# Mixer B of a hybrid decoder step: bias loads moved ahead of each stage's last loop turn, one group merge moved into the next round's first GEMM, small cache copies spread over the FFN stages

## The chip, the cores and the metric

The kernel runs on one core of one Trainium2 chip. The metric is the device time of one execution in microseconds (us); lower is better. Engine names are those of the profile: PE is TensorE (PEld its weight loads), DVE is VectorE, ACT is ScalarE, POOL is GpSimd, SP is SyncE, which here only issues DMAs.

## The reference

One inference step of a two-layer decoder over 512 prompt tokens and 8 x 4 sampled tokens, all in float32. Each layer is a half-step SwiGLU FFN, a token mixer and a second half-step FFN, each followed by a LayerNorm. Layer 0 has mixer A (sliding-window attention with sinks), layer 1 has mixer B: three groups of heads with window and dilation (128, 1), (512, 4) and (2048, 16), whose outputs are combined by their softmax denominators.

```python
for i in range(DEPTH):                      # DEPTH = 2
    xp, xs = half_ffn(xp, i, 0, 0), half_ffn(xs, i, 0, 0)
    ...                                     # mixer A (i = 0) or mixer B (i = 1)
    xp, xs = post_norm(xp, yp, i, 1), post_norm(xs, ys, i, 1)
    xp, xs = half_ffn(xp, i, 1, 2), half_ffn(xs, i, 1, 2)

def mixer_b_prompt(x, w_qkv, w_o, table):
    qkv = (x @ w_qkv).reshape(b, s, N_GROUPS_B, 3, N_HEADS, HEAD_DIM)
    for gi, (w, d) in enumerate(DILATED_GROUPS):
        ...                                 # banded attention with stride d: o and log-sum-exp
    y = combine_groups(outs, lses).reshape(b, s, -1) @ w_o

def combine_groups(outs, lses):
    w = jax.nn.softmax(jnp.stack(lses, 0), axis=0)
    return jnp.einsum('gnth,gnthd->nthd', w, jnp.stack(outs, 0))
```

For the sampled tokens, the caches of past keys and values (the oldest four rows dropped, four new ones appended) are outputs too. So nearly all cache bytes are copied from input to output in HBM: the long ones (groups 2 and 3 of mixer B) and the small ones, 128 rows per sequence (group 1 of mixer B, 8 KB a row, and mixer A, 2 KB a row).

## The kernel before

All work is laid out by hand, engine by engine, with semaphores between the engines. The work is a list of phases: for each layer `up`, `down`, `qkv`, `wo`, `up`, `down`. A phase is a row of units. One unit is one weight tile of 128 output columns: SP loads it into one of four buffers `raw` (`load_unit`, DMA lines L555, L559, L564), ACT casts it into `wh` (L1215), DVE takes the rest into `wl` (L1476), and PE multiplies with both (L777, L779, L781), 48 matmuls of 272 columns in two PSUM banks. A buffer `raw[j]` is free again when the unit's `wl` is made; SP waits for that (`wl_rdy`) before each load. SP's queue is in program order, so whatever stands ahead of a load holds it up.

Mixer B has two rounds (8 heads each). A round has two stages. The first is a GEMM of 12 units for group 1 and its attention, the second a GEMM of 24 units for groups 2 and 3 and their attention. Round 0 is `qkv[1, 0, 0]` and `qkv[1, 0, 1]`, round 1 is `qkv[1, 1, 0]` and `qkv[1, 1, 1]`. Below they are stage 1, 2, 3 and 4. In a GEMM of a stage, PE transposes each finished tile (L920, and L921 for the sampled tokens' 32 columns, once a tile), DVE and ACT in turn stage the tile and keep the transposed part (`stage_tile`, `keep_tokens`). Each attention (`attention(ps, rn)`) needs a bias of 1 MB in `RB["bias"]`; the buffer is single, so `load_bias` waits until the attention before it has added its last bias.

After a round's second attention the two slots `RB["o"][0]` and `RB["o"][1]` are merged: POOL sends each slot's maxima and denominators through HBM to swap their token order (`exchange`, `fetch`), DVE and ACT make the weights (`weights(k)`, L1634 to L1647), and `outputs_b(r)` puts features on partitions. PE transposes four pairs (L1018, 8 transposes each, into banks 6 and 7), ACT copies bank 6 (L1366), DVE adds bank 7 (L1667), and PE waits for that before it starts the next pair.

For each of the four mixer B stages SP does this before:

```python
load_bias(pass_b[2 * ph.run.rnd + (ph.run.items[0][1] > 0)])
n0 = 4 * ph.run.rnd + 2 * (ph.run.items[0][1] > 0)
keep_small(1, n0, n0 + 2)
keep_small(0, n0, n0 + 2)
load_units(ph, 1)
```

Units 0 to 3 are loaded before that (`load_first`). `keep_small` copies the small caches of two sequences, from HBM to HBM. The long caches are copied in the FFN phases, one DMA behind each weight load (`keep`, `keep_rows`, L539). The four `up` phases have 44 units each, eleven loop turns of four.

Of the kernel before, what the change touches and what calls it, by code (L numbers as in the profile page):

```python
# [20 lines left out]
P = 128  # L21
D_MODEL = 1024
KC = D_MODEL // P
SEQ = 512
NS = 8
DEC = 4
# [6 lines left out]
DEPTH = 2  # L33
# [74 lines left out]
def build(nc, t, o):  # L108
# [4 lines left out]
    with ExitStack() as ctx:  # L113
# [412 lines left out]
        def _(sp):  # L526
# [13 lines left out]

            def keep_small(layer, n0, n1):

                src = caches[layer, 0][0, n0:n1].rearrange("n r w h d -> n (r w h d)")
                dst = states_s[layer, 0][0, n0:n1].rearrange("n r w h d -> n (r w h d)")
                row = 2 * LAYER[layer]["kv"] * HD
                total = src.shape[1]
                sp.dma_start(dst[:, 0:total - DEC * row], src[:, DEC * row:total]).then_inc(copy_done[2 * DEPTH], 16)

# [35 lines left out]

            def load_units(ph, first):
                with sp.Fori(first, ph.units // RAW) as it:
                    for j in range(RAW):
                        load_unit(ph, it, j)
                        keep(ph, it, j)
                    if ph is up[0, 0]:  # L590
                        sp.wait_ge(line_o, 32)
                        repeat_lines(it * LINE_ROWS, LINE_ROWS)
# [126 lines left out]
            for ph in phases:  # L719
                if ph is qkv[0]:  # L720
                    load_qkv_a(ph, range(RAW))
                    load_bias(pass_a)
                    load_qkv_a(ph, range(RAW, ph.units))
                elif ph.kind == "qkv":
                    if not peeled:
                        load_first(ph)
                    load_bias(pass_b[2 * ph.run.rnd + (ph.run.items[0][1] > 0)])
                    n0 = 4 * ph.run.rnd + 2 * (ph.run.items[0][1] > 0)
                    keep_small(1, n0, n0 + 2)
                    keep_small(0, n0, n0 + 2)  # L730
                    load_units(ph, 1)
                else:
                    if ph.kind == "down" and ph.l == 0:
                        load_first(ph)
                        if ph.f == 0:
                            load_norms()
                            repeat_lines(LINE_ITS * LINE_ROWS, P - LINE_ITS * LINE_ROWS)
                        load_decode_constants(ph.f)
                        for j in range(RAW):
                            keep(ph, 0, j)  # L740
                        load_units(ph, 1)
                    else:
                        load_units(ph, peeled)
# [15 lines left out]
            for f in range(2 * DEPTH):  # L759
                sp.wait_ge(copy_done[f], 16 * RAW * (UP_ITS + DOWN_ITS))  # L760
            sp.wait_ge(copy_done[2 * DEPTH], 16 * 2 * 4)
            sp.wait_ge(new_done, 16 * 4)
# [8 lines left out]
        def _(pe):  # L771
# [338 lines left out]
            for ph in phases:  # L1110
# [10 lines left out]
                elif ph.kind == "qkv":  # L1121
                    qkv_run(ph, n_norm)
                    if ph is qkv[0]:
                        attention(pass_a, ph.run)
                        outputs_a()
                        decode(0)
                    else:
                        r, y = ph.run.rnd, int(ph.run.items[0][1] > 0)
                        attention(pass_b[2 * r + y], ph.run)
                        if y:  # L1130
                            outputs_b(r)
                            if r:
                                pe.wait_ge(sp_l, 2)
                                decode(1)
                            else:
                                pe.wait_ge(ot_v, PAIRS + 4)
                else:
# [72 lines left out]
        def _(act):  # L1210
# [94 lines left out]
            def run(ph):  # L1305
                r = ph.run
                for i in range(r.n):
# [50 lines left out]
            def outputs_b(r):  # L1358
# [3 lines left out]
                for p_ in range(4):  # L1362
                    act.wait_ge(ot_done, PAIRS + 4 * r + p_ + 1)
                    if p_ >= 2:
                        act.wait_ge(ot_v, PAIRS + 4 * r + p_ - 1)
                    act.copy(RB["st"][p_ % 2][:, 0:SEQ], bank[6][:]).then_inc(ot_a, 1)  # L1366
                if r:
# [72 lines left out]
            for ph in phases:  # L1440
                if ph.kind == "qkv":
# [6 lines left out]
                    else:  # L1448
                        r, y = ph.run.rnd, int(ph.run.items[0][1] > 0)
                        attention(pass_b[2 * r + y], ph.run)  # L1450
                        if y:
                            weights(1 + 2 * r)
                            weights(2 + 2 * r)
                            outputs_b(r)
                            if r:
                                decode(1)
                elif ph.kind == "up":
# [11 lines left out]
        def _(dve):  # L1469
# [110 lines left out]
            def run(ph):  # L1580
                r = ph.run
                for i in range(r.n):
# [45 lines left out]
            def weights(k):  # L1628
# [29 lines left out]
            def outputs_b(r):  # L1658
# [3 lines left out]
                for p_ in range(4):  # L1662
                    dve.wait_ge(ot_a, PAIRS + 4 * r + p_ + 1)
                    v = RB["at"][:, p_, :].rearrange("p (u c) -> p u c", c=4)
                    y = bank[7][:].rearrange("p (c u) -> p u c", c=4)
                    x = RB["st"][p_ % 2][:, 0:SEQ].rearrange("p (u c) -> p u c", c=4)
# [163 lines left out]
            for ph in phases:  # L1830
                if ph.kind == "qkv":
# [13 lines left out]
                    else:  # L1845
                        r, y = ph.run.rnd, int(ph.run.items[0][1] > 0)
                        attention(pass_b[2 * r + y], ph.run)
                        if y:
                            ps = pass_b[2 * r + 1]
                            dve.wait_ge(st_done, ps.u0 + ps.units)  # L1850
                            dve.wait_ge(oev_done, ps.u0 + ps.units + 2)
                            weights(1 + 2 * r)
                            weights(2 + 2 * r)
                            outputs_b(r)
                            if r:
                                decode(1)
                elif ph.kind == "up":
# [227 lines left out]
```

## Time and profile before

| | before |
|---|---|
| time, median of 3 runs | 3385.55 us (3382.94 to 3388.15) |
| the profiled execution | 3389.92 us, span 3388.1 us |
| PE busy | 2939.0 us, 87% of the span |
| PEld busy | 2669.2 us, 79% |
| DVE, ACT, POOL busy | 1286.1, 895.1 and 820.6 us (38%, 26%, 24%) |
| mean granted PE clock | 0.918 |
| DMA | 482.09 MB; SP's queue takes 42.0% of 16 engines' span |
| time on this kernel's four mixer B stages (from 1696 to 2538 us) | about 842 us |

PE is busy for most of the span, so the time hangs on its pauses. The four FFN stretches show hardly any. The page's slices of granted clock dip in the mixer stages and in the two decodes. How each pause came about is read from the waits, the timeline of an engine, and the DMAs.

### The profile page before, as it was taken

The numbers are of one execution on the slowest core, as the hardware profiler recorded it, in microseconds if no ns is written. First come the engines' busy times: TensorE is split into PE (matmuls) and PEld (weight loads), VectorE is DVE, ScalarE is ACT, GpSimd is POOL, SyncE is SP. The second block draws the span as 40 slices with busy tenths as digits, with TensorE's granted clock in tenths as the row PEclk, the third lists the DMA queues.
The fourth block names the chain that finished last, engine by engine and source line by source line (L and its number), as shares of the span: only waits on it lengthen the run. The fifth ranks groups of instructions, "written<-read, shape, count | busy, mean of one in ns | idle before, by whom it ended". The sixth has DMA issues, their size and how long they took to land. (4 is left out here: it accounts for less than half of the span.)

```text
span 3388.1 us, 53741 instructions
## 1 busy us (share of the span) xinstructions
PE 2939.0 (87%) x20802; PEld 2669.2 (79%) x20802; DVE 1286.1 (38%) x1934; ACT 895.1 (26%) x1725; POOL 820.6 (24%) x834
## 2 busy tenths in 40 slices
PE   8999998548999999999968696786964787899998
PEld 7999987417899999999967696776952222899998
DVE  2222244673422224222234123341258665422223
ACT  2222123432222222222124123131233341322212
POOL 2222012251222202222012123111226552122210
PEclk9999999758999999999979898898975888999999
DMA  7666431003566535665221231213305676366651
GB/s 244 228 236 180 154 82 30 17 15 93 187 206 200 186 124 180 208 207 186 90 94 52 95 108 54 76 54 100 107 8 174 245 278 250 101 206 206 211 170 49
DMA packets 466743, 482.09 MB, mean 142 GB/s; under 512 B 60878, under 2 KB 439871, under 8 KB 462448
## 3 DMA queue, kind: packets, MB, share of 16 engines
q1 hardware_dynamic: 456584, 467.46, 42.0%
q0 software_dynamic: 6416, 12.20, 1.3%
q8 instruction: 85, 1.39, 0.2%
q10 hardware_dynamic: 3616, 0.69, 0.1%
q14 instruction: 42, 0.34, 0.0%
HBM read 466.46 MB, written 199.42 MB: 197 GB/s over the span
## 5 line engine op out<-in xcount | busy, mean ns | idle before, releaser
L777 PE MATMUL bank<-sb_xh,sb_wl 128*128 128x272 f32 x4416 | 962.6, 295 | 124.8 <-DVE sb_wl L1476 102.5
L781 PE MATMUL bank<-sb_xh,sb_wh 128*128 128x272 f32 x4416 | 949.4, 292 | 0.0
L779 PE MATMUL bank<-sb_xl,sb_wh 128*128 128x272 f32 x4416 | 946.2, 291 | 0.0
L1476 DVE TENSOR_TENSOR sb_wl<-sb_raw,sb_wh 128x1024 fp32r<-128x1024 f32 (+1 forms) x340 | 453.4, 1334 | 1109.5 <-ACT sb_wh L1215 1100.9
L777 PEld LDWEIGHTS bank<-sb_xh,sb_wl 128*128 128x128 f32 x4416 | 717.4, 192 | 133.3 <-issue 76.1
L779 PEld LDWEIGHTS bank<-sb_xl,sb_wh 128*128 128x128 f32 x4416 | 717.8, 192 | 0.7
L781 PEld LDWEIGHTS bank<-sb_xh,sb_wh 128*128 128x128 f32 x4416 | 712.3, 192 | 0.0
L1215 ACT CAST sb_wh<-sb_raw 128x1024 fp32r<-128x1024 f32 (+1 forms) x340 | 376.5, 1110 | 1048.5 <-PE bank L781 939.3
L1898 POOL CAST sb_hh<-sb_h 128x544 f32 x88 | 130.2, 1480 | 758.2 <-DVE sb_h L1485 758.2
L777 PE MATMUL bank<-sb_hh,sb_wl 128*128 128x272 f32 x1408 | 311.4, 292 | 0.0
L781 PE MATMUL bank<-sb_hh,sb_wh 128*128 128x272 f32 x1408 | 304.2, 288 | 0.0
L779 PE MATMUL bank<-sb_hl,sb_wh 128*128 128x272 f32 x1408 | 303.7, 287 | 0.0
L777 PEld LDWEIGHTS bank<-sb_hh,sb_wl 128*128 128x128 f32 x1408 | 226.4, 188 | 2.0
L779 PEld LDWEIGHTS bank<-sb_hl,sb_wh 128*128 128x128 f32 x1408 | 225.8, 188 | 0.5
L781 PEld LDWEIGHTS bank<-sb_hh,sb_wh 128*128 128x128 f32 x1408 | 225.1, 188 | 0.0
L2005 POOL TENSOR_TENSOR sb_dprb<-sb_dkvb,sb_dqbb 128x1024 f32<-128x1024 f32 x64 | 168.1, 2639 | 108.1 <-ACT sb_dqbb L1386 71.1
L1485 DVE TENSOR_TENSOR sb_h<-sb_sil,bank 128x272 f32<-128x272 f32 x176 | 69.0, 433 | 267.8 <-PE bank L781 267.8
L1039 PE MATMUL bank<-sb_dq2b,sb_pick 128*128 128x512 f32 x192 | 93.5, 563 | 73.5 <-ACT sb_dqbb L1386 54.9
L1039 PEld LDWEIGHTS bank<-sb_dq2b,sb_pick 128*128 128x128 f32 x192 | 39.2, 225 | 148.3 <-ACT sb_dqbb L1386 113.1
L1222 ACT ACTIVATE sb_sil<-bank 128x272 f32<-128x272 f32 x88 | 35.0, 398 | 441.6 <-PE bank L781 441.6
L1069 PE MATMUL bank<-sb_dkvb,sb_dpb 128*16 128x512 f32 x384 | 139.0, 680 | 12.7 <-DMA sb_dkvb<-in_cache_b_kv 12.0
L1781 DVE TENSOR_REDUCE sb_dsb<-sb_dprb 128x16 f32<-128x1024 f32 x96 | 114.8, 1217 | 58.1 <-POOL sb_dprb L2005 56.9
(244 smaller groups left out, 2774.1 us busy)
## 6 DMA issues: line engine op xcount, KB each, us to landing
out_state_b_s<-in_cache_b_kv SPq DMA_DIRECT2D x176, 704.0 KB, 6.2
sb_dkvb<-in_cache_b_kv SPq DMA_DIRECT2D x144, 512.0 KB, 5.7
sb_raw<-in_ffn_w_gate SPq DMA_DIRECT2D x88, 512.0 KB, 3.8
sb_raw<-in_ffn_w_up SPq DMA_DIRECT2D x88, 512.0 KB, 4.2
sb_raw<-in_ffn_w_down SPq DMA_DIRECT2D x64, 704.0 KB, 4.6
sb_raw<-in_attn_b_w_qkv SPq DMA_DIRECT2D x72, 512.0 KB, 3.9
out_state_b_s<-in_cache_b_kv SPq DMA_DIRECT2D x32, 1016.0 KB, 7.6
out_state_b_s<-in_cache_b_kv SPq DMA_DIRECT2D x4, 1984.0 KB
```

Source lines behind the costliest of these rows:

```text
L777: pe.matmul(acc(s, h), wl[slot][:, k, :], hi(k)[:, halves[h]], start=start and k == 0, stop=False)
L779: pe.matmul(acc(s, h), wh[slot][:, k, :], lo(k)[:, halves[h]], start=False, stop=False)
L781: last = pe.matmul(acc(s, h), wh[slot][:, k, :], hi(k)[:, halves[h]], start=False, stop=end)
L1039: pe.matmul(bank[c][:], pick[:, tok:tok + 1].to_broadcast([P, P]), D["q2"][:, y.g, c * 512:(c + 1) * 512], start=True, stop=True).then_inc ...
L1069: mm = pe.matmul(bank[2 + 4 * (n % 2) + c][32 * tau:32 * tau + HEADS, 0:w], D["p"][:, g, n * DEC + tau, :], D["kv"][x.slot][:, c * w:(c + ...
L1215: act.copy(wh[j % 2][:, 0:ph.chunks, :], raw[j][:, 0:ph.chunks, :]).then_inc(wh_rdy, 1)
L1222: act.activation(sil[b][:, halves[0]], acc(0, 0), ACT.Silu)
L1476: dve.tensor_tensor(wl[j % 2][:, 0:ph.chunks, :], raw[j][:, 0:ph.chunks, :], v.bitcast(F32), ALU.subtract).then_inc(wl_rdy, 1)
L1485: last = dve.tensor_tensor(h32[b][:, halves[h]], sil[b][:, halves[h]], acc(1, h), ALU.mult)
L1781: dve.tensor_reduce(D["s"][:, y.g, tok * HEADS:(tok + 1) * HEADS], D["pr"][y.slot][:].rearrange("p (h d) -> p h d", d=HD), AX_X, ALU.add). ...
L1898: pool.tensor_copy(hi, h32[b][:]).then_inc(hh_rdy, 1)
L2005: pool.tensor_tensor(D["pr"][y.slot][:].rearrange("p (k r d) -> p k r d", r=rep, d=HD), kk, D["qb"][y.slot][:].rearrange("p (k r d) -> p k ...
```

## The change

Three things are changed.

1. In the mixer stages the bias is loaded before the last loop turn's four weight units, and no longer behind the first four units. In mixer A (a stage of 12 single units) it moves from behind unit 3 to behind unit 7.
2. `keep_small` is gone. `keep_window` copies the same rows in pieces: eleven rows of two sequences of both small caches at the end of each turn of an `up` phase, and the last three rows in the `down` phase. All `down` phases now load their first four units ahead of their copies.
3. Round 0's merge is taken out of the end of stage 2. Its weights are made by DVE and ACT in stage 3's GEMM, behind tiles 3 and 6, and `outputs_b(0)` runs behind that GEMM, ahead of stage 3's attention. In both rounds `outputs_b` now uses banks 6 and 7 for even pairs and banks 4 and 5 for odd ones, and PE waits only for the pair before the last.

```diff
-            def keep_small(layer, n0, n1):
-
-                src = caches[layer, 0][0, n0:n1].rearrange("n r w h d -> n (r w h d)")
-                dst = states_s[layer, 0][0, n0:n1].rearrange("n r w h d -> n (r w h d)")
-                row = 2 * LAYER[layer]["kv"] * HD
-                total = src.shape[1]
-                sp.dma_start(dst[:, 0:total - DEC * row], src[:, DEC * row:total]).then_inc(copy_done[2 * DEPTH], 16)
+            def keep_window(ffn, r0, rows):
+
+                n = slice(2 * ffn, 2 * ffn + 2)
+                for layer in range(2):
+                    src = caches[layer, 0][0, n].rearrange("n r w h d -> n r (w h d)")[:, bass.ds(r0 + DEC, rows), :]
+                    dst = states_s[layer, 0][0, n].rearrange("n r w h d -> n r (w h d)")[:, bass.ds(r0, rows), :]
+                    sp.dma_start(dst, src).then_inc(copy_done[2 * DEPTH], 16)
...
+            def load_units(ph, first, end=None):
+                with sp.Fori(first, end or ph.units // RAW) as it:
                     for j in range(RAW):
                         load_unit(ph, it, j)
                         keep(ph, it, j)
+                    if ph.kind == "up":
+                        keep_window(ph.ffn, it * LINE_ROWS, LINE_ROWS)
...
                 elif ph.kind == "qkv":
                     if not peeled:
                         load_first(ph)
+                    last = ph.units // RAW - 1
+                    load_units(ph, 1, last)
                     load_bias(pass_b[2 * ph.run.rnd + (ph.run.items[0][1] > 0)])
-                    n0 = 4 * ph.run.rnd + 2 * (ph.run.items[0][1] > 0)
-                    keep_small(1, n0, n0 + 2)
-                    keep_small(0, n0, n0 + 2)
+                    load_units(ph, last, last + 1)
...
             def outputs_b(r):
                 pe.wait_ge(ow_rdy, NBLK + 8 * (r + 1))
                 for p_ in range(4):
-                    if p_:
-                        pe.wait_ge(ot_v, PAIRS + 4 * r + p_)
+                    if p_ >= 2:
+                        pe.wait_ge(ot_v, PAIRS + 4 * r + p_ - 1)
...
-                            mm = pe.transpose(bank[6 + y][:, b * P:(b + 1) * P], RB["o"][y][:, b, p_ * P:(p_ + 1) * P], ident[:])
+                            mm = pe.transpose(bank[6 - 2 * (p_ % 2) + y][:, b * P:(b + 1) * P], RB["o"][y][:, b, p_ * P:(p_ + 1) * P], ident[:])
...
+                        if r and not y:
+                            for b in range(2):
+                                pe.wait_ge(tr_free[b], (ph.run.tr0 + ph.run.n) // 2 + 2)
+                            outputs_b(0)
+                            pe.wait_ge(ot_v, PAIRS + 4)
                         attention(pass_b[2 * r + y], ph.run)
-                        if y:
-                            outputs_b(r)
-                            if r:
-                                pe.wait_ge(sp_l, 2)
-                                decode(1)
-                            else:
-                                pe.wait_ge(ot_v, PAIRS + 4)
+                        if r and y:
+                            outputs_b(1)
+                            pe.wait_ge(sp_l, 2)
+                            decode(1)
...
+                    if ph is qkv[1, 1, 0] and i in (3, 6):
+                        weights(i // 3)
...
+                    if ph is qkv[1, 1, 0] and i in (3, 6):
+                        group_weights(0, i // 3 - 1)
...
+            def group_weights(r, y):
+
+                ps = pass_b[2 * r + 1]
+                dve.wait_ge(st_done, ps.u0 + ps.units)
+                dve.wait_ge(oev_done, ps.u0 + ps.units + 2)
+                weights(1 + 2 * r + y)
```

The first addition with `i in (3, 6)` is ACT's, the second DVE's. The order of the instructions on three engines follows. Line numbers are those of each kernel's own file, so a line that did not change has another number in the change.

**SP, stage 1 of mixer B, before.** The four loads of the first row are units 0 to 3, `sb_biasb` is the bias, L547 are the two small copies (the shape is that of the whole transfer, in float32 elements), and the last rows begin the loop over the other units.

```order
L564 DMA sb_raw<-in_attn_b_w_qkv 128x8x128 x4
L636 DMA sb_biasb<-scr_lines_x 128x8x256
L547 DMA out_state_b_s<-in_cache_b_kv 2x16x15872
L547 DMA out_state_a_s<-in_cache_a_kv 2x4x15872
L586 UNCONDITIONAL_BRANCH
L586 ISA
L564 ISA
L564 DMA sb_raw<-in_attn_b_w_qkv 128x8x128
```

**SP, the same place in the change.** Each row of four loads is one turn.

```order
L564 DMA sb_raw<-in_attn_b_w_qkv 128x8x128 x4
L586 UNCONDITIONAL_BRANCH
L564 DMA sb_raw<-in_attn_b_w_qkv 128x8x128 x4
L586 REGISTER_ALU
L586 COMPARE_AND_BRANCH
L638 DMA sb_biasb<-scr_lines_x 128x8x256
L586 UNCONDITIONAL_BRANCH
L564 DMA sb_raw<-in_attn_b_w_qkv 128x8x128 x4
```

The two copies have left the stage, and units 4 to 7 stand ahead of the bias.

**SP, the end of a turn of an `up` phase, in the change.** Before, the turn ends with the copy of L539 behind the fourth load.

```order
L555 DMA sb_raw<-in_ffn_w_up 128x8x128
L539 ISA
L539 DMA out_state_b_s<-in_cache_b_kv 16x11264
L547 ISA x2
L547 DMA out_state_a_s<-in_cache_a_kv 2x5632
L547 ISA
L547 DMA out_state_b_s<-in_cache_b_kv 2x2x11264
L586 REGISTER_ALU
```

The long copy is laid out as 16 pieces, the two new ones have the two sequences as their outermost dimension.

**DVE, from stage 2's last attention rows on, before.** L1612 is the attention's output, L1634 to L1647 are one slot's weights, L1667 the sums of `outputs_b`, L1476 makes `wl` of the next GEMM (stage 3). The second slot's weights, the same nine rows, are left out.

```order
L1612 COPY sb_ob<-bank 128x128 x3
L1634 TENSOR_TENSOR sb_tb<-sb_mdb,sb_mob 128x32
...
L1647 TENSOR_TENSOR sb_ob<-sb_ob,sb_tb 128x512 x4
...
L1667 TENSOR_TENSOR sb_at<-bank,sb_stb 128x512 x4
L1476 TENSOR_TENSOR sb_wl<-sb_raw,sb_wh 128x1024 x2
L1181 COPY sb_stb<-bank 128x272
```

**DVE, stage 3's GEMM in the change.** L1483 makes `wl`, L1185 to L1208 are `stage_tile` and `keep_tokens`, L1643 to L1656 a slot's weights.

```order
L1483 TENSOR_TENSOR sb_wl<-sb_raw,sb_wh 128x1024 x2
L1185 COPY sb_stb<-bank 128x272
L1186 COPY sb_stb<-bank 128x272
L1208 COPY sb_ssb<-bank 32x128
L1643 TENSOR_TENSOR sb_tb<-sb_mdb,sb_mob 128x32
...
L1656 TENSOR_TENSOR sb_ob<-sb_ob,sb_tb 128x512 x4
L1483 TENSOR_TENSOR sb_wl<-sb_raw,sb_wh 128x1024 x2
```

One slot's weights now stand between tile 3's copies and the `wl` of units 5 and 6; the other slot's stand between the `wl` of unit 7 and that of unit 8.

**PE, from stage 2's attention (L992) into stage 3's GEMM, before.**

```order
L976 MATMUL bank<-sb_ident,sb_stb 128x128 x4
L992 MATMUL bank<-sb_vb,sb_ktb 128x128 x8
L1018 MATMUL bank<-sb_ident,sb_ob 128x128 x32
L777 MATMUL bank<-sb_xh,sb_wl 128x272 x2
L779 MATMUL bank<-sb_xl,sb_wh 128x272 x2
```

**PE, from stage 3's last transposes of tiles (L922, L923) into its attention (L968), in the change.**

```order
L922 MATMUL bank<-sb_ident,sb_stb 128x128 x4
L923 MATMUL bank<-sb_ident,sb_stb 32x128
L1020 MATMUL bank<-sb_ident,sb_ob 128x128 x32
L968 MATMUL bank<-sb_kb,sb_qsb 128x128 x2
L968 MATMUL bank<-sb_kb,sb_qsb 128x256 x2
```

The 32 transposes of round 0's merge have moved from the head of stage 3's GEMM to its end.

## Rows read from the trace of the kernel before

**Rows 1.** Waits from 1696 to 2876 us: total us, times, longest us.

```profile
ACT sb_wh L1215 <- DMA sb_raw<-in_attn_b_w_qkv: 87.2, 6, 30.2
PE bank L777 <- DVE sb_wl L1476: 77.6, 5, 26.5
PE bank L1018 <- DVE sb_ob L1647: 42.6, 2, 29.8
```

**Rows 2.** PE's timeline around unit 4 of stages 1, 2 and 4.

```profile
1735.16 0.27 PE L921 MATMUL bank<-sb_ident,sb_stb 128*32 128x128 f32 x1
...
1765.84 0.27 PE L921 MATMUL bank<-sb_ident,sb_stb 128*32 128x128 f32 x1
...
1772.40 0.27 PE L921 MATMUL bank<-sb_ident,sb_stb 128*32 128x128 f32 x1
...
1886.74 0.27 PE L921 MATMUL bank<-sb_ident,sb_stb 128*32 128x128 f32 x1
...
1922.60 0.27 PE L921 MATMUL bank<-sb_ident,sb_stb 128*32 128x128 f32 x1
...
2298.64 0.27 PE L921 MATMUL bank<-sb_ident,sb_stb 128*32 128x128 f32 x1
...
2333.14 0.27 PE L921 MATMUL bank<-sb_ident,sb_stb 128*32 128x128 f32 x1
```

**Rows 3.** DMAs issued 1702.5 to 1703.5 us: KB each, median us to landing.

```profile
sb_raw<-in_attn_b_w_qkv SPq DMA_DIRECT2D x1, 512.0 KB, 51.5
```

**Rows 4.** DMA queue, 1709 to 1748 us: packets, MB, share of 16 engines.

```profile
q1 hardware_dynamic: 36, 2.16, 12.8%
```

**Rows 5.** Windows 902 to 926 and 2101 to 2131 us: busy times, PEclk, DMA share, GB/s.

```profile
902.00:926.00 24.00, 24.00 (x194) 24.00 (x193) 6.42 (x9) 5.34 (x8) 6.04 (x4) 1.00 0.62 208
2101.00:2131.00 30.00, 0.26 (x2) 0.28 (x3) 8.59 (x25) 0.70 (x4) 1.30 (x2) 0.54 0.21 76
```

**Rows 6.** PE's timeline, into stage 2 and into stage 3.

```profile
1861.07 0.49 PE L777 MATMUL bank<-sb_xh,sb_wl 128*128 128x272 f32 x2 [0.54 <-issue]
...
1873.62 0.27 PE L921 MATMUL bank<-sb_ident,sb_stb 128*32 128x128 f32 x1
...
2098.97 2.03 PE L992 MATMUL bank<-sb_vb,sb_ktb 128*128 128x128 f32 x16
...
2134.08 1.97 PE L1018 MATMUL bank<-sb_ident,sb_ob 128*128 128x128 f32 x8 [1.40 <-DVE sb_at L1667]
...
2158.43 0.27 PE L921 MATMUL bank<-sb_ident,sb_stb 128*32 128x128 f32 x1
```

**Rows 7.** DVE's timeline, weights of round 0 and stage 3's tile 3.

```profile
2120.86 0.19 DVE L1634 TENSOR_TENSOR sb_tb<-sb_mdb,sb_mob 128x32 f32<-128x32 f32 x1 [19.54 <-DMA sb_mob<-scr_md]
...
2125.69 0.18 DVE L1634 TENSOR_TENSOR sb_tb<-sb_mdb,sb_mob 128x32 f32<-128x32 f32 x1
...
2171.33 0.44 DVE L1181 COPY sb_stb<-bank 128x272 f32<-128x272 f32 x1 [3.56 <-PE bank L781]
...
2172.47 1.40 DVE L1476 TENSOR_TENSOR sb_wl<-sb_raw,sb_wh 128x1024 fp32r<-128x1024 f32 x1 [0.16 <-ACT sb_wh L1215]
```

**Rows 8.** PE's timeline, the start of stage 3's attention.

```profile
2228.68 1.89 PE L966 MATMUL bank<-sb_kb,sb_qsb 128*128 128x128 f32 x8 [3.26 <-POOL sb_qsb L1963]
```

**Rows 9.** ACT's and DVE's timelines, a pair of `outputs_b(1)`.

```profile
2532.85 0.59 ACT L1366 COPY sb_stb<-bank 128x512 f32<-128x512 f32 x1 [2.79 <-PE bank L1018]
...
2533.47 0.69 DVE L1667 TENSOR_TENSOR sb_at<-bank,sb_stb 128x512 f32<-128x512 f32 x1 [2.68 <-ACT sb_stb L1366]
```

**Rows 10.** DMAs issued 858 to 1120 us, an `up` phase: KB each, us to landing.

```profile
out_state_b_s<-in_cache_b_kv SPq DMA_DIRECT2D x38, 704.0 KB, 6.2
sb_raw<-in_ffn_w_gate SPq DMA_DIRECT2D x19, 512.0 KB, 3.8
```

**Rows 11.** SP's issue and ACT's cast of the same buffer in an `up` turn.

```profile
902.39 0.38 SPq L555 DMA_DIRECT2D sb_raw<-in_ffn_w_gate  x1
...
923.93 1.05 ACT L1215 CAST sb_wh<-sb_raw 128x1024 fp32r<-128x1024 f32 x1
```

More of the change, by code:

```diff
@@ L583, in keep @@
                     keep_rows(2, 2 * ph.ffn + j % 2, it * DOWN_ROWS + UP_ITS * 2 * UP_ROWS, DOWN_ROWS, ph.ffn)
-            def load_units(ph, first):
-                with sp.Fori(first, ph.units // RAW) as it:
+            def load_units(ph, first, end=None):
+                with sp.Fori(first, end or ph.units // RAW) as it:
                     for j in range(RAW):
@@ L720, in _ @@
                 if ph is qkv[0]:
-                    load_qkv_a(ph, range(RAW))
+                    load_qkv_a(ph, range(2 * RAW))
                     load_bias(pass_a)
-                    load_qkv_a(ph, range(RAW, ph.units))
+                    load_qkv_a(ph, range(2 * RAW, ph.units))
                 elif ph.kind == "qkv":
@@ L726, in _ @@
                         load_first(ph)
+                    last = ph.units // RAW - 1
+                    load_units(ph, 1, last)
                     load_bias(pass_b[2 * ph.run.rnd + (ph.run.items[0][1] > 0)])
-                    n0 = 4 * ph.run.rnd + 2 * (ph.run.items[0][1] > 0)
-                    keep_small(1, n0, n0 + 2)
-                    keep_small(0, n0, n0 + 2)
+                    load_units(ph, last, last + 1)
+                elif ph.kind == "down":
+                    load_first(ph)
+                    if ph.l == 0 and ph.f == 0:
+                        load_norms()
+                        repeat_lines(LINE_ITS * LINE_ROWS, P - LINE_ITS * LINE_ROWS)
+                    if ph.l == 0:
+                        load_decode_constants(ph.f)
+                    keep_window(ph.ffn, UP_ITS * LINE_ROWS, BLK - DEC - UP_ITS * LINE_ROWS)
+                    for j in range(RAW):
+                        keep(ph, 0, j)
                     load_units(ph, 1)
                 else:
[L733 to L741, printed above, removed]
-                    else:
-                        load_units(ph, peeled)
+                    load_units(ph, peeled)
                 peeled = int(ph.kind == "qkv")
@@ L760, in _ @@
                 sp.wait_ge(copy_done[f], 16 * RAW * (UP_ITS + DOWN_ITS))
-            sp.wait_ge(copy_done[2 * DEPTH], 16 * 2 * 4)
+            sp.wait_ge(copy_done[2 * DEPTH], 16 * 2 * 2 * DEPTH * (UP_ITS + 1))
             sp.wait_ge(new_done, 16 * 4)
@@ L1365, in outputs_b @@
                         act.wait_ge(ot_v, PAIRS + 4 * r + p_ - 1)
-                    act.copy(RB["st"][p_ % 2][:, 0:SEQ], bank[6][:]).then_inc(ot_a, 1)
+                    act.copy(RB["st"][p_ % 2][:, 0:SEQ], bank[6 - 2 * (p_ % 2)][:]).then_inc(ot_a, 1)
                 if r:
@@ L1449, in _ @@
                         r, y = ph.run.rnd, int(ph.run.items[0][1] > 0)
+                        if r and not y:
+                            outputs_b(0)
                         attention(pass_b[2 * r + y], ph.run)
[L1451 to L1456, printed above, removed]
+                        if r and y:
+                            weights(3)
+                            weights(4)
+                            outputs_b(1)
+                            decode(1)
                 elif ph.kind == "up":
@@ L1664, in outputs_b @@
                     v = RB["at"][:, p_, :].rearrange("p (u c) -> p u c", c=4)
-                    y = bank[7][:].rearrange("p (c u) -> p u c", c=4)
+                    y = bank[7 - 2 * (p_ % 2)][:].rearrange("p (c u) -> p u c", c=4)
                     x = RB["st"][p_ % 2][:, 0:SEQ].rearrange("p (u c) -> p u c", c=4)
@@ L1846, in _ @@
                         r, y = ph.run.rnd, int(ph.run.items[0][1] > 0)
+                        if r and not y:
+                            outputs_b(0)
                         attention(pass_b[2 * r + y], ph.run)
[L1848 to L1856, printed above, removed]
+                        if r and y:
+                            group_weights(1, 0)
+                            group_weights(1, 1)
+                            outputs_b(1)
+                            decode(1)
                 elif ph.kind == "up":
```

1 line of the change is left out of this document (removed).

## The prediction

> **What bounds the kernel now.** I began with the waits of PE, since PE is busy 87% of the span and everything else has room. In the stretch of mixer B three waits stand out [rows 1]. PE waits 77.6 us for `wl` of a GEMM, five times, the longest 26.5. It waits 42.6 us for the merged slots, twice, the longest 29.8. And ACT, which makes `wh` ahead of `wl`, waits 87.2 us for weights to land. So the first wait is not DVE's or ACT's work: it is a late DMA. PE's timeline gives the place. One L921 ends each tile, and in a steady GEMM they are 6.56 us apart (1765.84 to 1772.40). Around unit 4 of stages 1, 2 and 4 the distance is 30.68, 35.86 and 34.50 us [rows 2]. Stage 3 has no such gap, as it begins with the merge.
>
> Then the DMAs. The load of unit 4 stands behind the bias and the two small copies, and landed 51.5 us after its issue [rows 3], where the weight loads of an `up` phase take 3.8 [rows 10]. Between 1709 and 1748 us SP's queue moved 36 packets, 2.16 MB, at 12.8% of 16 engines [rows 4]. That is two engines of 16, about 60 KB a packet, 55.4 GB/s together or 27.7 GB/s each. The two copies hold 1984 + 496 = 2480 KB, 1240 KB for each of two engines, which at 27.7 GB/s is 45.8 us. The weight tile is spread over all 16, so it is whole only when the two slow engines come to it. This explains all three gaps, and in stage 3 the copies lie under the merge wait.
>
> **The change part by part.**
>
> *Copies out of the mixer stages, loads ahead of the bias.* Unit 4's load needs only unit 0's buffer, which is free before PE starts the stage's GEMM, and nothing is left in front of it. I take the three gaps down to the steady distance: 30.68 - 6.56 = 24.1, 35.86 - 6.56 = 29.3, 34.50 - 6.56 = 27.9 [rows 2]. These differences also hold what the first GEMM after a pause loses on a lower clock. Sum 81.3 us. The bias now comes with the last turn, four units (26 us) ahead of its attention. It is 1 MB, twice a weight tile, so two to three times 3.8 us: its cover is at least twice that. If it were late the DVE, and with it PE, would wait for the difference. The bounds are 0 (something else holds unit 4) and 81.3.
>
> *Round 0's merge.* Stage 2's attention ends at 2098.97 + 2.03 = 2101.00 and the first L921 of stage 3 is at 2158.43, 57.43 us later. At the border of stages 1 and 2, where nothing is merged, it is from 1861.07 - 0.54 = 1860.53 to 1873.62, 13.09 us [rows 6]. So 57.43 - 13.09 = 44.3 us leave this place. Some of it comes back:
>
> (a) `outputs_b(0)` behind stage 3's GEMM. PE idles 3.26 us there anyway, while POOL stages the queries [rows 8]. A pair is 8 transposes, 1.97 us [rows 6] at a granted clock near half (0.54 in the idle stretch before, [rows 5]), so about 1.1 at full clock, then ACT's copy 0.59 and DVE's sum 0.69 [rows 9], with some 0.1 us per handover. With the last tile's copy ahead (0.8 us), pairs 0 and 1 go at once, pair 2 starts when pair 0 is summed (3.4 us), pair 3 at 4.5 and ends 2.6 later: 7.1 us, less the 3.26 that were idle, +3.9. Bounds: 0, and 11.0 if nothing overlaps (0.8 + 4 x 3.37 - 3.26, with 1.97 + 1.40 of [rows 6]).
>
> (b) The weights in the GEMM. One slot takes DVE 2125.69 - 2120.86 = 4.83 us. Tile 3's GEMM ends at 2171.3, its copies take to 2172.4, and then `wl` of unit 5 took 1.2 to 1.4 us [rows 7]. With a slot between, `wl` is there 1.1 + 4.8 + 1.25 = 7.15 us after the tile's end, and PE wants it after 6.56 + 0.3: late by 0.3. What is queued behind it on DVE (tile 5's copies) has a unit's time. The second slot begins earlier, behind unit 7's `wl`, but needs ACT's exponentials, and ACT stands at tile 6's staging until that GEMM ends. By the same count `wl` of unit 8 comes 6.9 us after tile 6, late by 0.1. Sum +0.5, bounds 0 and 2 x 4.83 = 9.7.
>
> So 44.3 - 3.9 - 0.5 = 39.9.
>
> *`outputs_b(1)` with four banks.* Before, four pairs of 1.97 + 1.40 = 3.37 us, 13.5 [rows 6]. Here PE is slow after its wait, so the transposes come one behind the other, 4 x 1.97 = 7.9, plus the last pair's 0.59 + 0.69 and handovers: 9.3. Decode waits for the end of it: 4.2 us gained; bounds 0 and 5. The wait ahead (the second of [rows 1], 12.8 of the 42.6) stays.
>
> *Copies in the `up` phases.* Per turn two more DMAs, from 22 rows of 8 KB and 22 rows of 2 KB. They are issued with the two sequences outermost, as the old ones were, so I charge them to two engines: 110 KB each, 112.6 KB at 27.7 GB/s = 4.1 us per turn. A turn lasts 24 us with a DMA share of 0.62 [rows 5], or 14.9 us of each engine; with 4.1 it is 19.0, so no backlog is carried over. A load issued at 902.39 lands 3.8 later, and its buffer's next cast is at 923.93 [rows 10, 11]: 17.7 us of cover against 4.1. I take 0. If that cover were gone it would cost up to 44 turns x 4.1 = 179 us. Two more issues on SP, about 0.7 us each, fit into its waits. The long copies, spread over 16 engines, land in 6.2 us [rows 10] and nobody waits for them.
>
> The Trainium skill, *DMA: Bandwidth & Descriptors*, section "Why a DMA increments its semaphore by 16 and not by 1", says that the number of engines follows from the slowest dimension other than 1 of both access patterns, the largest divisor up to 16. By that rule a leading 2 means two engines, and the trace agrees for the old copies (12.8% of 16). It speaks against the change, since the new ones have it too, always on the same two engines. The sum would be the same by it, unless the cover in the `up` phases fails.
>
> *Mixer A's bias behind unit 7* is covered, as PE has no gap there now: 0. *Down phases*: four loads ahead of their copies, 0.
>
> **Sum.** 81.3 + 39.9 + 4.2 = 125.4 us. The profiled execution took 3389.9 us (span 3388.1 and 1.8 around it): 3264.5. It lies 4.4 us above the median of the runs, 3385.55, so I forecast **3260 us**.
>
> **Rivals.**
>
> *The merge is not hidden* (bounds of (a) and (b)): DVE's two slots stand fully in PE's way and the pairs run one by one: +7.1 and +9.2 us, 3276. For it: DVE has hardly 4 us of slack per unit. Against: the count above leaves PE only 0.4 late. Chance 7%.
>
> *Something else holds unit 4.* The change takes the copies away and the loads stay late, say because SP stands at another semaphore. Then only the merge and the banks count: 3385.6 - 44.1 = 3341. Against: the 51.5 us are from issue to landing, not before the issue. Chance 3%.
>
> *Slower: the small copies hold the weights of the `up` phases.* Two engines get 4.1 us more per turn on top of 14.9. Should each turn stand by more than 125.4 / 44 = 2.85 us, the change loses; with the whole 4.1 on the path the time is 3260 + 179 = 3439. That needs loads to land more than 20 us after issue, and the rows give 3.8. Chance 2%.
>
> *Forecast case*: 87%, own range 3250 to 3270. The rest, 1%, is no change.
>
> **The range.** From 3250 (nothing comes back from (a) and (b), and 5 us of run-to-run and size) to 3280, which takes in the first rival. Faster by over 0.2% (7 us, about what a measurement of this kernel can tell from none) 0.97, same 0.01, slower 0.02.
>
> **What would show it.** Right: L921 every 6.56 us through units 3 to 5 of all four stages; unit 4's load landing in about 4 us; no wait of PE for ACT's or DVE's data of 20 us; stage 3's first L921 13 us after stage 2's attention; between stage 3's last tile and its scores some 7 us with 32 transposes; `up` turns still 24 us. Wrong: a gap of PE at units 5 or 8 of stage 3 over 1 us, gate or up loads that land later than 15 us, or a wait of DVE for the bias ahead of an attention.

## The result, and the profile after

The changed kernel takes **3258.09 us** (median of 4 runs, 3254.3 to 3262.15); the kernel before, run beside it on the same chip, 3385.12 us (3382.94 to 3388.15). The ratio is 0.9622, its 95% interval 0.961 to 0.9634: 127 us less. The profiled execution took 3262.15 us with a span of 3260.3 us, where before had 3389.92 and 3388.1; its mean granted clock is 0.939 (0.918).

The waits of PE in mixer B, 1696 to 2746 us (columns as in [rows 1]):

```profile
PE bank L978 <- ACT sb_stb L1336: 20.1, 29, 1.7
PE bank L1041 <- DVE sb_dq2b L1694: 17.0, 1, 17.0
PE bank L1020 <- DVE sb_ob L1656: 12.9, 1, 12.9
...
PE bank L963 <- POOL sb_qsb L1977: 8.7, 2, 4.4
...
PE bank L779 <- DVE sb_wl L1483: 3.9, 3, 2.0
```

Against [rows 1]: the wait for `wl` has gone from 77.6 to 3.9 us, that for the merged slots from 42.6 in two pieces to 12.9 in one. ACT's 87.2 us for weights to land has no row left in this stretch. L923 is the L921 of [rows 2]; PE's timeline of stage 1:

```profile
1728.78 0.27 PE L923 MATMUL bank<-sb_ident,sb_stb 128*32 128x128 f32 x1
1735.34 0.27 PE L923 MATMUL bank<-sb_ident,sb_stb 128*32 128x128 f32 x1
1741.90 0.27 PE L923 MATMUL bank<-sb_ident,sb_stb 128*32 128x128 f32 x1
```

Every 6.56 us, where [rows 2] has 30.68 at this place. The DMAs issued from 1698 to 1740 us show why, 3.7 us instead of the 51.5 of [rows 3], and the bias beside them:

```profile
sb_raw<-in_attn_b_w_qkv SPq DMA_DIRECT2D x5, 512.0 KB, 3.7
sb_biasb<-scr_lines_x SPq DMA_DIRECT2D x1, 1024.0 KB, 6.9
```

PE's timeline from the last product of stage 2 into stage 3, the only pause in that GEMM (unit 5), and from its last transposes into the attention:

```profile
2045.30 2.03 PE L994 MATMUL bank<-sb_vb,sb_ktb 128*128 128x128 f32 x16
2047.86 0.49 PE L779 MATMUL bank<-sb_xh,sb_wl 128*128 128x272 f32 x2 [0.54 <-issue]
...
2060.39 0.27 PE L923 MATMUL bank<-sb_ident,sb_stb 128*32 128x128 f32 x1
...
2080.70 0.52 PE L779 MATMUL bank<-sb_xh,sb_wl 128*128 128x272 f32 x2 [0.35 <-DVE sb_wl L1483]
...
2127.73 0.27 PE L923 MATMUL bank<-sb_ident,sb_stb 128*32 128x128 f32 x1
2128.87 1.94 PE L1020 MATMUL bank<-sb_ident,sb_ob 128*128 128x128 f32 x16 [0.87 <-DVE sb_ssb L1208]
2131.34 1.97 PE L1020 MATMUL bank<-sb_ident,sb_ob 128*128 128x128 f32 x16 [0.53 <-DVE sb_at L1683]
2134.71 1.58 PE L968 MATMUL bank<-sb_kb,sb_qsb 128*128 128x128 f32 x8 [1.40 <-DVE sb_at L1683]
```

From the end of the attention (2047.33) to the first L923 it is 13.06 us, where [rows 6] has 57.43. The merge's 32 transposes go in two groups of 16: two pairs at once, then each after the sum of the one before the last.

In an `up` phase the windows show the window copies as a somewhat larger DMA share, 0.64 at 882 to 906 us where [rows 5] has 0.62 for a like turn. The DMAs issued from 858 to 1120 us, with their queue's total (packets, MB, share of 16 engines):

```profile
q1 hardware_dynamic: 46935, 52.53, 59.9%
...
out_state_b_s<-in_cache_b_kv SPq DMA_DIRECT2D x38, 704.0 KB, 6.2
...
out_state_b_s<-in_cache_b_kv SPq DMA_DIRECT2D x10, 176.0 KB
out_state_a_s<-in_cache_a_kv SPq DMA_DIRECT2D x10, 44.0 KB
```

Against [rows 10], the long copies land as before, and the gate weights in 4.0 us instead of 3.8.

**The balance of the two spans**, from the first and the last matmul of each stage in both timelines: GEMMs of stages 1, 2 and 4: -24.1, -29.3 and -28.0; stage 3's border and GEMM -43.8; from there to its attention +3.4, and that attention -2.1; stage 4's attention -1.7; from its end to the decode -5.1; the decode, from its first to its last product of queries and cached keys, +2.9. Sum -127.8 = 3260.3 - 3388.1. The parts that are not listed moved as well, by up to 2 us each (the last `up` GEMM -1.9, mixer A's attention -1.4), and cancel.

### The profile page after: what moved, and what is told of

It reads as the page before. It is cut to its first block and busy times, and to the rows that moved or that the text cites. A ratio compares the mean times of both kernels' runs of the same rounds, so it can differ in the third digit from the quotient of the medians.

```text
span 3260.3 us, 54005 instructions
## 1 busy us (share of the span) xinstructions
PE 2920.5 (90%) x20802; PEld 2648.9 (81%) x20802; DVE 1284.9 (39%) x1934; ACT 894.0 (27%) x1725; POOL 817.0 (25%) x834
## 5 line engine op out<-in xcount | busy, mean ns | idle before, releaser
L1483 DVE TENSOR_TENSOR sb_wl<-sb_raw,sb_wh 128x1024 fp32r<-128x1024 f32 (+1 forms) x340 | 453.0, 1333 | 1001.7 <-ACT sb_wh L1219 992.8
```

The costliest lines, as they stand in the source:

```text
L1483: dve.tensor_tensor(wl[j % 2][:, 0:ph.chunks, :], raw[j][:, 0:ph.chunks, :], v.bitcast(F32), ALU.subtract).then_inc(wl_rdy, 1)
```

## The experiments

Times are medians; "before" beside each is its run on the same chip.

**The copies alone.** In the kernel before, `keep_small` gives way to `keep_window` in the FFN stages; bias, merge and banks stay.

```diff
+                    if ph.kind == "up":
+                        keep_window(ph.ffn, it * LINE_ROWS, LINE_ROWS)
...
                     load_bias(pass_b[2 * ph.run.rnd + (ph.run.items[0][1] > 0)])
...
-                    keep_small(1, n0, n0 + 2)
-                    keep_small(0, n0, n0 + 2)
                     load_units(ph, 1)
...
```

> The kernel before with only the small copies moved into the FFN phases; the bias is still ahead of unit 4, the merge and the banks are as before. Theory (the two-engine copies held unit 4's load): the gaps of stages 1, 2 and 4 go (-81.3 us), and round 0's merge wait falls from 29.8 us to the 12.9 of round 1, since its exchange through HBM is not held either (-16.9): about 3385 - 98 = 3287 us, 3280 to 3295. Rival (the bias, or SP's wait for it ahead of unit 4, holds the load): the gaps stay in full or in half, 3330 us or more.

Measured: 3286.56 us (before 3387.52), ratio 0.9713 (0.9697 to 0.973): 101 us less. All GEMM gaps are gone. Of the two merge waits round 0's is shorter, 16.2 us instead of 29.8 (I had expected 12.9); round 1's stays at 12.8:

```profile
PE bank L1020 <- DVE sb_ob L1649: 29.0, 2, 16.2
```

**The copies stay, but spread over 16 engines.** One DMA for each sequence; source and target are then one row of numbers each, without the dimension of two sequences.

```diff
-                src = caches[layer, 0][0, n0:n1].rearrange("n r w h d -> n (r w h d)")
+                for n in range(n0, n1):
+                    src = caches[layer, 0][0, n].rearrange("r w h d -> (r w h d)")
...
```

> The kernel before with each small copy issued per sequence, 16 pieces each (992 KB and 248 KB), in the same place ahead of unit 4. Theory (it is the two engines, not the bytes or the place): 2480 KB over 16 engines at 27.7 GB/s are 5.7 us, unit 4's load lands within about 15 us, well inside its 26 us: as the copies-only kernel, 3287 us, 3280 to 3300. Rival (2.4 MB of HBM traffic ahead of the load is the cause, wherever it runs): unit 4 late as before, 3370 us or more.

Measured: 3291.89 us (before 3387.52), ratio 0.9728 (0.971 to 0.9745): 96 us less without moving a DMA. The same bytes stand in front of unit 4's load, and it lands 11 us after its issue. The DMAs issued from 1700 to 1712 us:

```profile
sb_raw<-in_attn_b_w_qkv SPq DMA_DIRECT2D x2, 512.0 KB, 11.4
out_state_b_s<-in_cache_b_kv SPq DMA_DIRECT2D x1, 992.0 KB, 9.2
```

The packets of the large copy have the same size in both traces, 63,488 bytes. Before, they run two at a time, each 2.34 us long, from 1705 to 1752 us; here 16 start between 1701.9 and 1703.4 us. So it was the two engines that held the weights, not the bytes, the packets or the order as such. It stays 5 us above the copies-alone run; 4 of the 5 are in the merge waits, 33.1 us in sum instead of 29.0.

**The merge alone**, with its four banks; SP's part as before.

```diff
+                        if r and not y:
...
+                            outputs_b(0)
...
-                    if p_:
-                        pe.wait_ge(ot_v, PAIRS + 4 * r + p_)
+                    if p_ >= 2:
+                        pe.wait_ge(ot_v, PAIRS + 4 * r + p_ - 1)
```

> The change without its SP part: merge in stage 3's GEMM and four banks, copies and bias ahead of unit 4 as before. Theory (in stage 3 the copies' hold lay under the merge wait): a gap of 25 to 29 us appears at unit 4 of stage 3. The gain is 44.3 - 4.4 + 4.2 - 27.9 = 16 us: 3369 us, 3360 to 3376. Rival (the parts add up one by one): -44, 3341 us.

Measured: 3367.5 us, ratio 0.995 (0.9934 to 0.9967): 20 us less. The merge leaves the place where it hid stage 3's copies, and unit 4 of stage 3 now waits like that of the other stages:

```profile
2151.46 0.81 PE L777 MATMUL bank<-sb_xh,sb_wl 128*128 128x272 f32 x2 [25.57 <-DVE sb_wl L1481]
```

Its GEMM is 27 us longer than in the change (105.55 us, 78.49).

**The order alone.** Bias and both small copies, laid out as before, ahead of the last loop turn.

```diff
+                    last = ph.units // RAW - 1
+                    load_units(ph, 1, last)
                     load_bias(pass_b[2 * ph.run.rnd + (ph.run.items[0][1] > 0)])
                     keep_small(1, n0, n0 + 2)
                     keep_small(0, n0, n0 + 2)
-                    load_units(ph, 1)
+                    load_units(ph, last, last + 1)
```

> The kernel before with bias and whole small copies together moved ahead of the last loop turn; nothing else. Theory: the two slow engines now hold the first unit of the last turn (unit 8 or 20). It is issued some 4 us after the tile six units before it ended, lands 51 us later and is wanted 39.7 us after that tile's end: a gap of about 18 us in each of the four stages, 72 us in place of 81.3, and the merge wait falls by 16.9: 3359 us, 3345 to 3375. Rival (the place of the bias was what held the loads): gaps gone, 3287 us or less.

Measured: 3378.36 us (10 runs), ratio 0.9976 (0.9966 to 0.9985). The prediction took copies and order as one step; of the order alone only 9 us come. The gaps move to the first unit of the last turn, 19.4, 22.3, 20.5 and 22.8 us, and there are four of them, stage 3's too. With what PE loses behind them (last section) the four GEMMs are 93.5 us longer than steady ones, more than the 81.4 of before; what is gained is round 0's merge wait, 12.8 us instead of 29.8. My 3359 missed by 19: I had expected 72 us for the four gaps, they are 85.0, and 8.5 us come behind them. The load behind the copies still takes long:

```profile
sb_raw<-in_attn_b_w_qkv SPq DMA_DIRECT2D x1, 512.0 KB, 47.2
```

**SP's part whole**, the copies in the FFN stages and the bias ahead of the last turn, on the other engines of before. The edit is the SP part of the change's diff.

> The whole of the change's SP part (copies in the FFN stages, bias ahead of the last loop turn) on the kernel before's other engines: both merges stay as they were, with two banks. It differs from the run with the copies alone (3286.56 us) only in the place of the bias. Theory (the bias behind units 0 to 3 holds nobody once the copies behind it are gone, and ahead of the last turn it holds nobody either): within 3 us of that run, 3284 to 3290, ratio to before 0.970 to 0.972, no gap of PE in the GEMMs. Rival: 1 MB of bias in front of the last four weight tiles makes the first of them late: some 5 us in each stage, 3300 or more, with a PE gap at the first unit of the last turn.

Measured: 3286.81 us (before 3386.32), ratio 0.9709 (0.9696 to 0.9722), as the copies alone: the time shows nothing of the bias's place. The profile shows where the prediction's split was off. PE's wait for round 0's merge is no longer the 29.8 of [rows 1]; the first row is of PE, the second of DVE, from 2040 to 2075 and 2040 to 2080 us:

```profile
PE bank L1020 <- DVE sb_ob L1649: 12.7, 1, 12.7
```

```profile
DVE sb_tb L1636 <- DMA sb_mob<-scr_md: 2.5, 1, 2.5
```

In [rows 7] DVE waited 19.54 us for the same `sb_mob`, which comes over HBM behind stage 3's copies. That wait is 2.5 here: 17 us of the merge wait were not the merge's. Most of them go with the copies alone, where DVE waits 5.9 us and PE 16.2; the last 3.4 go with the bias and unit 4's load, which with the copies alone are issued beside this exchange (at 2038.5 and 2039.2 us) and with SP's part whole are not. Other parts of the two kernels differ by as much, so the time doesn't show them.

**Two banks.** The change, with `outputs_b` on banks 6 and 7 alone and a wait for each pair.

```diff
-                    if p_ >= 2:
-                        pe.wait_ge(ot_v, PAIRS + 4 * r + p_ - 1)
+                    if p_:
+                        pe.wait_ge(ot_v, PAIRS + 4 * r + p_)
...
```

> The change with the old outputs_b: two banks, each pair waits for the one before; the merge stays behind stage 3's GEMM. Theory: in stage 3 a pair takes about 1.1 + 1.4 = 2.5 us on the full clock, 10 us in place of 7.1, +3; in round 1 the 4.2 us come back. So 3258 + 7 to 8 = 3266 us, 3260 to 3271. Rival (PE's end of the pairs is hidden behind POOL's and ACT's work): 3258, no difference.

Measured: 3267.18 us (before 3387.55), ratio 0.965 (0.9634 to 0.9666), 9 us above the change. PE's timeline has the 3.37 us pitch of [rows 6] back:

```profile
2125.99 1.97 PE L1020 MATMUL bank<-sb_ident,sb_ob 128*128 128x128 f32 x8 [1.40 <-DVE sb_at L1683]
2129.36 1.97 PE L1020 MATMUL bank<-sb_ident,sb_ob 128*128 128x128 f32 x8 [1.40 <-DVE sb_at L1683]
```

Round 0's merge takes 11.17 us on PE instead of 4.44, round 1's 12.23 instead of 6.67: 12.3 in the two stages. The medians differ by 9; their ratios' intervals (0.9634 to 0.9666, 0.961 to 0.9634) only just part, so the timeline is the stronger evidence, and the 9 are a rough size.

**The window copies doubled, and tripled.** For each small copy of an `up` or `down` phase one or two more of the same rows into scratch, which nobody reads. These runs do more work than the reference asks.

```diff
                     sp.dma_start(dst, src).then_inc(copy_done[2 * DEPTH], 16)
+                    for m in range(1):
+                        sp.dma_start(junk_d[m][layer][n, bass.ds(r0, rows), :], src).then_inc(junk_done, 16)
```

> The change, where every small window copy of the FFN phases is issued twice, the second time into a scratch region of HBM (work added, outputs the same). Theory (cover): two engines get 8.1 us a turn on top of 14.9, 23.0 of 24 us: no backlog, 3258 us, 3252 to 3268. Rival (copies on two engines hold the loads of each turn for as long as they run): +4.1 x 44 = +179, 3437 us; or at least tens of us.

> As the doubled one, but two scratch copies beside the real one. Theory: 14.9 + 12.2 = 27.1 us a turn for two engines, over the 24 that a turn has. The backlog grows by 3.1 us a turn, eats the 17.7 us of cover after six turns and then stretches the turns: some 16 us for each of three up phases and 32 for the first one, whose DMAs are busier, about 80 us: 3338 us, 3290 to 3380. Rival (the two engines have no part in the loads' time): 3258, no difference.

Measured: 3254.05 us (3251.99 to 3256.25), ratio 0.9608 (0.9592 to 0.9624), with one more: no cost. (It ends 4 us below the change, but up to the end of round 1's merge the two profiles are level, at 2404.99 and 2404.95 us.) With two more 3307.83 us, ratio 0.9765 (0.9749 to 0.9782), 50 above the change. The DMAs issued from 858 to 1120 us, first with one more, then with two:

```profile
q1 hardware_dynamic: 47020, 54.77, 63.3%
...
out_state_b_s<-in_cache_b_kv SPq DMA_DIRECT2D x38, 704.0 KB, 7.3
sb_raw<-in_ffn_w_gate SPq DMA_DIRECT2D x19, 512.0 KB, 5.5
```

```profile
out_state_b_s<-in_cache_b_kv SPq DMA_DIRECT2D x37, 704.0 KB, 8.8
sb_raw<-in_ffn_w_gate SPq DMA_DIRECT2D x19, 512.0 KB, 8.1
```

And ACT's waits with two more, from 1 to 450 us (the first `up` and `down`), where the change has 15.9 us for the down weights and no row of the other two:

```profile
ACT sb_wh L1224 <- DMA sb_raw<-in_ffn_w_gate: 28.5, 6, 6.5
ACT sb_wh L1224 <- DMA sb_raw<-in_ffn_w_down: 22.8, 3, 14.8
ACT sb_wh L1224 <- DMA sb_raw<-in_ffn_w_up: 14.5, 6, 2.8
```

The first `up` GEMM is 17 us longer, the first two `down` ones 12 and 9; the others change by 0 to 2. I had expected 3338, from a backlog that grows by 3.1 us a turn and costs 32 us in the first `up` phase and 16 in each other. SP's timeline in the first one, with two more and then in the change:

```profile
165.37 8.69 SPq L541 DMA_DIRECT2D out_state_b_s<-in_cache_b_kv  x1
...
192.81 8.83 SPq L541 DMA_DIRECT2D out_state_b_s<-in_cache_b_kv  x1
```

```profile
165.16 0.53 SPq L539 DMA_DIRECT2D out_state_b_s<-in_cache_b_kv  x1
```

With two more a turn takes 27.44 us, near the 27.1 of the estimate, where the change has 23.94. SP spends the time in the issue of a turn's first long copy, 8.7 us instead of about 0.5. The landing times count from the issue and so don't grow: a turn's first load lands 13.2 to 14.5 us after it, in the second turn as in the last. In the second `up` phase SP still waits 56.8 us for free buffers, so it keeps up, and there the estimate was too high.

**The window copies spread over 16 engines**, one DMA for each sequence and layer.

```diff
-                n = slice(2 * ffn, 2 * ffn + 2)
+                for n in range(2 * ffn, 2 * ffn + 2):
```

> The change with the window copies issued per sequence in 16 pieces, so twice as many DMAs, spread over all engines. Theory: the two engines' 4.1 us a turn are covered, so spreading them buys nothing, and two more issues of SP a turn cost nothing: 3258 us, 3252 to 3264. Rival (some loads are late by a little in each turn): 3250 or less.

Measured: 3258.81 us, ratio 0.962 (0.9604 to 0.9636), as the change. In the `up` phases two engines are good enough.

**A version that beats both.** POOL stages the first two query blocks of each attention ahead of the last two `store_out`s, not behind them.

```diff
-                    if i:
+                    if i and i < r.n - 1:
                         store_out(r, i - 1)
-                store_out(r, r.n - 1)
...
+                    if blk == 2 and isinstance(i, int) and not i:
+                        store_out(rn, rn.n - 2)
+                        store_out(rn, rn.n - 1)
```

> The change, and on POOL's queue the query blocks 0 and 1 of each attention are staged ahead of the last two store_outs of tiles (four DMA issues, about 0.5 us each) instead of behind them. In the profile of the change PE waits 3.2 to 4.4 us for POOL's queries at the head of the attentions of mixer A and of stages 1, 2 and 4; in stage 3 the merge hides this. Theory (PE is held there by POOL's queue order, and every us there is on the path): about 2 us less in each of four places, 8 in sum: 3250 us (3245 to 3257), and a PE wait for queries of about 1.5 us where it was 3.3. Rival 1: PE then waits as long for something else that ends at the same time (the last tile's stage or its transposes): 3258, within 3 of the change. Rival 2: the stores that are now later hold the K and V reads that follow them: slower, 3262 or more.

Measured: **3241.19 us** (3239.88 to 3244.17, 5 runs; before 3386.32), ratio 0.9573 (0.956 to 0.9586): 17 us below the change, twice what I expected and outside my range. The first score of stage 1's attention, in the change and here:

```profile
1792.44 1.82 PE L968 MATMUL bank<-sb_kb,sb_qsb 128*128 128x128 f32 x7 [3.25 <-POOL sb_qsb L1977]
```

```profile
1787.37 1.55 PE L968 MATMUL bank<-sb_kb,sb_qsb 128*128 128x128 f32 x8 [1.13 <-ACT sb_ssb L1208]
```

That is the 2.1 us that I had counted, as in mixer A; in stages 2 and 4 the pause ahead of the attention is 3.2 us shorter, 10.7 in sum. I had counted 2 us for these two as well. What I had not counted is that the attentions behind are shorter too, by 1.7, 1.7 and 1.0 us in mixer A and stages 1 and 2 (0.6 longer in stage 4), and the pieces between an attention and its decode by 1.5 together: 16.0 us in sum. That the edit makes the attentions shorter is not shown: among the other kernels profiled, none of which touches them, the same three differ by 2.2 to 2.6 us. The two profiles differ by 21.4 us, 6.0 of them in mixer B's decode, which no edit touches. POOL's two issues for each tile cost 1.07 us of its time, and here those of the last tile lie under PE's first scores:

```profile
1787.55 0.51 POOL L1929 DMA_DIRECT2D scr_kvb<-sb_ssb  x1
1788.05 0.56 POOL L1939 DMA_DIRECT2D out_state_b_p<-sb_vb  x1
1788.65 1.29 POOL L1979 COPY sb_qsb<-sb_qb 64x128 f32<-64x128 f32 x4
```

## Why the prediction was right

The forecast was 3260, the result is 3258.09; in the profiled executions 125.4 us less were forecast and 127.8 came. By the steps of the prediction:

- **Copies out of the mixer stages, loads ahead of the bias**: predicted 81.3 us, measured 24.1 + 29.3 + 28.0 = 81.4. That the two engines of the copies were the cause, and not the queue as such, is shown from both sides: the same bytes over 16 engines at the same place gained 96 us where taking them away gained 101, the same DMAs on two engines at another place 9. Of the bias's own place, the other half of the step, the time shows nothing (3286.81 against 3286.56). The bias landed in 6.9 us, less than the two to three times 3.8 that I allowed for.
- **Round 0's merge**: 44.3 us less what comes back in the GEMM (0.5) is 43.8, and 43.8 was measured. Unit 5's `wl` is late by 0.35 us (predicted 0.3), unit 8's not at all (predicted 0.1; the two add up to 0.4, not to the 0.5 of the sum).
- **(a) `outputs_b(0)` behind the GEMM**: predicted +3.9, measured +3.4. From the last transposes to the scores it is 6.71 us, predicted 7.1. Not predicted: the attention behind is 2.1 us shorter, 41.6 us instead of 43.8. The cause is open: with the merge as before it takes 42.3 in the two runs without the copies, and with two banks, where its queries are staged as early as here, 43.0.
- **`outputs_b(1)` with four banks**: predicted -4.2, measured -5.1. The transposes take 6.67 us together, not 7.9, at a granted clock as low as before (0.55, before 0.54 from 2511 to 2538 us): run on without a break they take less than four times one pair's 1.97. The wait ahead stays at 12.9, as said.
- **Copies in the `up` phases**: predicted 0. By the two timelines the first three `up` GEMMs are as long as before to within 0.2 us, the last is 1.9 shorter, and the doubled copies cost nothing either. The estimate of 4.1 us per turn on two engines agrees with the share: 2.1 points (59.9 - 57.8%, the latter in the row below, of the kernel before) of 16 engines in 262 us are 88 us, over two engines and the ten turns whose copies lie in this window 4.4.

```profile
q1 hardware_dynamic: 46848, 50.28, 57.8%
```

- What was in none of the steps: stage 4's attention -1.7, the decode +2.9. The decode's code is the same; over the twelve kernels profiled here it takes 260.5 to 268.5 us (before 265.7), and the profiled execution of the change has the longest. It may make up most of its 4 us above the median; the other executions have no profile. That the unforeseen terms (-2.1, -1.7 and +2.9) nearly cancel is luck.

What the prediction had wrong is how it split the sum by cause. The rival "something else holds unit 4" took the merge and the banks alone for 44.1 us, 3341. Alone they gave 20 (3367.5), since with the merge gone stage 3 showed the gap of 27 us that had lain under it. Behind the removal of the copies they gave 29 (3286.8 to 3258.1), since 17 of the 29.8 us of the merge wait were a DMA (`sb_mob`) held up by other DMAs ([rows 7] has it, 19.54, and I passed over it; the expectations of the first runs already count it). So what a part is worth depends on the order: copies first, they give 99 us (3386.3 to 3286.8) and merge and banks 29, of which about 9 are the banks; merge and banks first, they give 20 and the copies 109. The forecast did not suffer, since it summed over places and not over causes.

The rival on the slow side is now measured: the copies on two engines cost nothing at twice their bytes and 50 us at three times. The signs that I gave for it hardly show it: even there no load lands over 20 us after its issue and few over 15 (at most 17.4), as the time goes into SP's issue, ahead of the landing's count. The Trainium skill, *DMA: Bandwidth & Descriptors*, section "Why a DMA increments its semaphore by 16 and not by 1", derives the number of engines from the slowest dimension other than 1; splitting off that dimension brought the load's landing from 51.5 to 11 us, in agreement with it.

## What to carry to other kernels

When a small load takes ten times its usual time, look at the DMA in front of it and count its engines (MB, time and share of 16 in the queue's row). Here a copy whose outermost dimension is 2 ran on two engines, and held up the load behind it at both places in the queue that were tried; such a copy should be spread, or cut into pieces that fit into the cover of a busy phase. Sum a forecast over places on the path, but ask for each wait what else ends with it: what looked like the merge's price was for 17 us that of DMAs beside it. When DMAs may be too many, look at how long their issue takes, and not only at the time from issue to landing. On an engine that both issues DMAs and stages data for PE, put the staging first.

## What the runs showed of the hardware

- The window copies doubled raised the share of the DMA engines by 3.4 points (59.9 to 63.3%), more than the 2.1 points of the first set for the same bytes: 142 us of engine time, 7.1 us per turn on each of two engines where the first set took 4.4. The long copies beside them landed in 7.3 instead of 6.2 us, and the packets of 45,056 bytes, of which they and the larger window copy consist, took 1.94 us each in the mean instead of 1.86: over the first 648 of them 52 of the 54 us of difference. So shares do not add up plainly.
- Where two engines have too much in hand, SP is held in the issue of a DMA: for the long copy of an `up` turn in the first two phases it takes 0.5 to 0.6 us in the kernel before, twice over 1 (at most 1.4), up to 2.1 in the change, 6.0 with the copies doubled and 9.3 with them tripled. With the window copies spread over 16 engines it is at most 0.8.
- A cost by overfull engines is not the same in like phases: with three sets the first `up` phase lost 17 us and the later ones 0 to 2. The first one has three more small copies in a turn (`scr_lines`); whether they set it apart was not tried.
- After a gap of some 20 us PE's next matmuls run slower (0.81 us for a pair in the merge-alone row above, 0.49 to 0.52 in the change), so a gap costs more than its idle time. The windows of the kernel before (columns as in [rows 5]) show the granted clock in stage 1's gap, in the 8 us behind it and after that; 1.00 is 2.4 GHz, and 0.5 would be the lower level of 1.2:

```profile
1735.00:1757.00 22.00, 0.50 (x5) 0.23 (x3) 1.42 (x2) 1.81 (x2) 0.00 (x0) 0.57 0.31 103
1757.00:1765.00 8.00, 8.00 (x45) 8.00 (x46) 1.82 (x4) 0.28 (x1) 2.17 (x2) 0.68 0.57 165
1765.00:1813.00 48.00, 47.66 (x386) 47.16 (x384) 14.48 (x23) 11.64 (x22) 9.22 (x17) 1.00 0.27 77
```

- The distances of L921 marks, which the prediction summed, hold this cost; the idle times that I counted for the order-alone experiment do not. It is 7.5 us for the three gaps of before (81.4 us of distance, 73.9 idle) and 8.5 for the four of the order-alone run (93.5, 85.0).
